# Feed-forward with context and latent tokens in tiles of their own, and tokens, weights and ring at one remainder modulo 512 bytes

## What is computed

```
h = rms_norm(x, norm2_gain) * (1.0 + sc2) + sh2
ff = square(relu(h @ w_ff1)) @ w_ff2
x = x + g2 * ff
y = rms_norm(x, final_gain)
```

## Time and profile before

| | |
|---|---|
| median of 3 runs | 1760.79 us (1759.97 to 1762.66) |
| the profiled execution's own time | 1762.74 us |
| its span, first to last instruction | 1761.0 us |
| TensorE busy | 1673.0 us, 95% |
| VectorE busy | 943.3 us, 54% |
| ScalarE busy | 650.0 us, 37% |

### The profile page before, as it was taken

How to read it: one execution, slowest core, us unless ns; L and a number is a source line. 1 busy time by engine, 2 the same in 40 slices (tenths; PEclk the granted TensorE clock), 3 DMA queues, 4 the chain that set the end, 5 groups by cost and what they waited for, 6 DMA issues and landing times.

```text
span 1761.0 us, 30968 instructions
## 1 busy us (share of the span) xinstructions
PE 1673.0 (95%) x13028; PEld 1399.8 (79%) x13028; DVE 943.3 (54%) x1355; ACT 650.0 (37%) x932; POOL 0.2 (0%) x4
## 2 busy tenths in 40 slices
PE   7799999889999999499999999999999999999997
PEld 5577787768777877497688888888878888888886
DVE  5712643653365346656686665666575444444436
ACT  3423236423643272417474445444442220122103
POOL 0000000000000000000000000000000000000000
PEclk7899999989999999699999999999999999999999
DMA  8454234323433243720052222222372220122102
GB/s 341 184 190 148 67 130 145 132 85 113 160 117 116 81 169 96 273 62 26 25 189 90 88 99 107 82 90 97 123 284 108 108 108 29 79 107 108 54 1 120
DMA packets 62270, 208.20 MB, mean 118 GB/s; under 512 B 8784, under 2 KB 17488, under 8 KB 60752
## 3 DMA queue, kind: packets, MB, share of 16 engines
q1 hardware_dynamic: 57120, 185.35, 29.1%
q10 hardware_dynamic: 5040, 21.22, 2.9%
HBM read 144.40 MB, written 62.13 MB: 117 GB/s over the span
## 4 chain that ended last, share of the span: by engine, by line
PE 49%; DVE 1%; DMA 1%; ACT 0%; issue 0%; SPq 0%; DVEq 0%
PE bank L95 16%; PE bank L97 16%; PE bank L96 16%; DMA hid_raw<-hidden 0%; PE bank L1269 0%; DVE hid_lo L1078 0%; DMA hidden<-c 0%; PE bank L711 0%; DVE x L1340 0%; DVE y_tok L1368 0%; DVE down_lo L1084 0%; DVE c L890 0%; DVE c L892 0%; PE bank L824 0%; SPq L1054 0%
## 5 line engine op out<-in xcount | busy, mean ns | idle before, releaser
L95 PE MATMUL bank<-h_hi,in_lo 128*128 128x512 f32 (+1 forms) x768 | 290.8, 379 | 12.1 <-issue 9.2
L96 PE MATMUL bank<-h_lo,in_hi 128*128 128x512 f32 (+1 forms) x768 | 277.8, 362 | 0.0
L95 PE MATMUL bank<-hid_hi,down_lo 128*128 128x512 f32 (+1 forms) x768 | 274.7, 358 | 3.0 <-DVE x L1340 1.5
L97 PE MATMUL bank<-h_hi,in_hi 128*128 128x512 f32 (+1 forms) x768 | 277.2, 361 | 0.0
L97 PE MATMUL bank<-hid_hi,down_hi 128*128 128x512 f32 (+1 forms) x768 | 273.1, 356 | 0.0
L96 PE MATMUL bank<-hid_lo,down_hi 128*128 128x512 f32 (+1 forms) x768 | 272.8, 355 | 0.0
L1340 DVE SCALAR_TENSOR_TENSOR x<-bank,mod,x 128x512 f32<-128x512 f32 (+1 forms) x216 | 142.1, 661 | 226.6 <-PE bank L97 226.5
L1698 ACT ACTIVATE mx_stage<-bank 128x512 f32<-128x512 f32 (+1 forms) x96 | 49.9, 523 | 351.8 <-PE bank L97 347.9
L95 PEld LDWEIGHTS bank<-h_hi,in_lo 128*128 128x128 f32 x768 | 149.1, 194 | 37.9 <-issue 14.9
L96 PEld LDWEIGHTS bank<-h_lo,in_hi 128*128 128x128 f32 x768 | 149.7, 195 | 24.4 <-issue 5.5
L97 PEld LDWEIGHTS bank<-h_hi,in_hi 128*128 128x128 f32 x768 | 149.4, 195 | 21.9
(11 more groups left out here) (233 smaller groups left out, 2601.3 us busy)
## 6 DMA issues: line engine op xcount, KB each, us to landing
proj<-mx_stage ACTq DMA_DIRECT2D x32, 640.0 KB, 5.7
hid_raw<-hidden SPq DMA_DIRECT2D x32, 640.0 KB, 7.1
in_raw<-in_w_in SPq DMA_DIRECT2D x32, 512.0 KB, 6.3
mx_ada_raw<-in_w_ada_rest SPq DMA_DIRECT2D x32, 512.0 KB, 5.1
up_raw<-in_w_ff SPq DMA_DIRECT2D x32, 512.0 KB, 4.3
hidden<-c SPq DMA_DIRECT2D x64, 256.0 KB, 2.0
down_raw<-in_w_ff SPq DMA_DIRECT2D x32, 512.0 KB, 7.2
ada<-in_w_ada SPq DMA_DIRECT2D x8, 1024.0 KB, 20.7
```

The costliest lines, as they stand in the source:

```text
L95: nc.tensor.matmul(out, w_lo, x_hi, start=start, stop=False)
L96: nc.tensor.matmul(out, w_hi, x_lo, start=False, stop=False)
L97: return nc.tensor.matmul(out, w_hi, x_hi, start=False, stop=stop)
```

## The change

No instruction is added, removed or moved on any engine. Only addresses of SBUF tiles change.

- `h2_hi` and `h2_lo` are each cut into a context tile (8 rows of 258 columns) and a latent tile (8 rows of 1024 columns). The context tiles are at 0 and 8.0625 KB, the latent ones at 16.125 and 48.125 KB.
- The ring tiles `hid2` to `hid7` and `down7` move up by 128 bytes, since `kb` now applies to them too.
- All readers and writers take the pair of tiles and pick one.

```
@@ -553,8 +553,6 @@
-    H = TOKENS + 2
-    AT = {0: 0, 1: CTX + 2}
@@ -579,8 +577,10 @@
-        self.h_hi, self.h_lo = at(nc, "h2_hi", [P, KT, self.H], F32R, 0), at(nc, "h2_lo", [P, KT, self.H], F32R, 40.0625)
-        self.h_raw = at(nc, "h2_raw", [P, KT, self.H], F32, 40.0625)
+        ctx, lat = [P, KT, CTX + 2], [P, KT, LAT]
+        self.h_hi = at(nc, "h2_ctx_hi", ctx, F32R, 0), at(nc, "h2_lat_hi", lat, F32R, 16.125)
+        self.h_lo = at(nc, "h2_ctx_lo", ctx, F32R, 8.0625), at(nc, "h2_lat_lo", lat, F32R, 48.125)
+        self.h_raw = at(nc, "h2_lat_raw", lat, F32, 48.125)
@@ -595,8 +595,8 @@
-        at_hid = lambda s: kb((120, 130)[s]) if s < 2 else 10 * (s - 2)
-        at_w = lambda s: (kb(168), kb(176), kb(140), kb(148), kb(156), kb(184), kb(192), 60)[s]
+        at_hid = lambda s: kb((120, 130)[s] if s < 2 else 10 * (s - 2))
+        at_w = lambda s: (kb(168), kb(176), kb(140), kb(148), kb(156), kb(184), kb(192), kb(60))[s]
@@ -641,15 +641,14 @@
     def columns(self, t, k, t0, n):
-        col = t0 if t0 < CTX else t0 + 2
-        return t[:, k, col:col + n]
+        return t[0][:, k, t0:t0 + n] if t0 < CTX else t[1][:, k, t0 - CTX:t0 - CTX + n]
...
-            return self.h_hi[:, rows, cols], self.h_lo[:, rows, cols]
+            return self.h_hi[1][:, rows, cols], self.h_lo[1][:, rows, cols]
@@ -771,7 +770,7 @@
-                             self.h_hi[:, k, 0:CTX + 2], self.h_lo[:, k, 0:CTX + 2], k == 0, k == KT - 1)
+                             self.h_hi[0][:, k, :], self.h_lo[0][:, k, :], k == 0, k == KT - 1)
@@ -792,9 +791,9 @@
-                t = slice(CTX + 2 + b * self.HALF, CTX + 2 + (b + 1) * self.HALF)
+                t = slice(b * self.HALF, (b + 1) * self.HALF)
                 last = exact_product(nc, g.bank[self.PLAIN_BANKS[s][b]][:, :], hi[:, s, cols], lo[:, s, cols],
-                                     self.h_hi[:, k, t], self.h_lo[:, k, t], k == 0, k == KT - 1)
+                                     self.h_hi[1][:, k, t], self.h_lo[1][:, k, t], k == 0, k == KT - 1)
```

More of the change, by code:

```diff
@@ L643, in columns @@
     def columns(self, t, k, t0, n):
-        col = t0 if t0 < CTX else t0 + 2
-        return t[:, k, col:col + n]
+        return t[0][:, k, t0:t0 + n] if t0 < CTX else t[1][:, k, t0 - CTX:t0 - CTX + n]
     def right(self, i):
-        a, b, first_half, last_half = slice(0, 4), slice(4, 8), slice(CTX + 2, CTX + 2 + self.HALF), slice(CTX + 2 + self.HALF, self.H)
+        a, b, first_half, last_half = slice(0, 4), slice(4, 8), slice(0, self.HALF), slice(self.HALF, LAT)
         rows, cols = {1: (a, first_half), 2: (b, first_half), 3: (b, last_half), 4: (a, last_half)}.get(i, (None, None))
         if rows is not None:
-            return self.h_hi[:, rows, cols], self.h_lo[:, rows, cols]
+            return self.h_hi[1][:, rows, cols], self.h_lo[1][:, rows, cols]
         return {5: (self.t_hi[0], self.t_lo[0]), 6: (self.t_hi[1], self.t_lo[1]), 7: (self.t_hi[2], self.t_lo[2])}[i]
@@ L681, in scalar_row @@
         if m == 0:
-            nc.scalar.activation(self.h_hi[:, :, self.SHIFT], g.mod[:, 24:32, :], ACT.Copy).then_inc(self.sh_hi, 1)
+            nc.scalar.activation(self.h_hi[0][:, :, self.SHIFT], g.mod[:, 24:32, :], ACT.Copy).then_inc(self.sh_hi, 1)
         for t0, n, c in SEGS:
@@ L695, in vector_row @@
             dve.wait_ge(self.sh_hi, 1)
-            nc.vector.tensor_tensor(self.h_lo[:, :, self.SHIFT], g.mod[:, 24:32, :], self.h_hi[:, :, self.SHIFT].bitcast(F32),
+            nc.vector.tensor_tensor(self.h_lo[0][:, :, self.SHIFT], g.mod[:, 24:32, :], self.h_hi[0][:, :, self.SHIFT].bitcast(F32),
                                     ALU.subtract).then_inc(self.sh_lo, 1)
@@ L1189, in combination_hi @@
             raw, hi = ((self.t_raw[i - 1], self.t_hi[i - 1]) if i < 4 else
-                       (self.h_raw[:, 0:4, CTX + 2 + self.HALF:], self.right(4)[0]))
+                       (self.h_raw[:, 0:4, self.HALF:], self.right(4)[0]))
             nc.scalar.activation(hi[:, :, :], raw[:, :, :], ACT.Copy).then_inc(self.t_hi_ready, 1)
@@ L1283, in vector @@
         t1, t2, t3 = self.t_raw
-        t4 = self.h_raw[:, 0:4, CTX + 2 + self.HALF:]
+        t4 = self.h_raw[:, 0:4, self.HALF:]
         def make(out, k, i, minus):
```

## The result

| | us |
|---|---|
| before, median of 5 runs | 1759.97 (1758.70 to 1762.66) |
| changed, median of 5 runs | 1750.58 (1747.72 to 1753.57) |
| ratio | 0.9941, 95% interval 0.9927 to 0.9954 |
| span of the profiled execution, before and after | 1761.0 and 1747.6 |

The change saves 9.4 us, a good half per cent. I had said 7.2 us and a time between 1751.3 and 1757.3. The direction and the mechanism held, and the size was too small.

What follows compares the result with a forecast made beforehand. TensorE was taken to bound all but the passage between up and down stages; 3.13 (up) + 0.24 (plain pair) + 2.98 + 0.62 + 0.24 (down) = 7.2 us, from 1760.79 to 1753.6 us, range 1751.3 to 1757.3.

Steps and rivals of the forecast that it cites:

- The bound and the cover: Up and down stages: TensorE is busy throughout and stays the bound; VectorE (237 of 377 us) and ScalarE (185) are not short.
- Two paces: 512-column matmuls: equal operand remainders modulo 512 bytes settle at 226.7 ns each, unequal ones stay at 231 to 234.
- Products 2 to 4: Up stage, 36 latent matmuls of a pair: run settled, 8.33 to 8.16 us, 0.17 saved a pair.
- the 258-column matmuls keep theirs, and a hand-over follows each context block: Up stage: context tiles keep old remainders; block 0 goes from 2.87 to 2.89 us, 0.02 lost a pair.
- Product 7: Up stage, after context block 1, reading t and s: shows the hand-over and stays at 2.76 us.
- Product 1: Up stage, 12 latent matmuls: becomes like product 7, 2.81 to 2.76 us, 0.05 saved a pair.
- The ring: Down stage, groups of four slots: every row at 6.90 us, from 6.993 and 6.926, saving 2.98 and 0.62 us.
- The last group: End of down stage: nine units of six go from 12.51 to 12.27 us, 0.24 saved; nothing counted behind them among transposes.
- The passage: Up to down stage, bound by a chain over VectorE, store and reload: still 40 us long, no gain counted.
- Half: Rival: settled pace holds in the ring but not the up stage; 3.84 us saved, 1757.0 us; chance 0.08.
- it doesn't do what it says: Rival: the remainder isn't the cause of the paces; time as before, 1760.8 us; chance 0.08.
- Slower: Rival: hand-over starts anew at each tile change, 2.6 us lost up, 5.1 down; 1768.5 us; chance 0.04.

Runs made afterwards that it cites:

- e4: Changed kernel with weight sums s 128 bytes above tokens, hid2 to hid5 256 and hid6, hid7 384 above their weights; product 5 2.80 us, slots 2 to 5 6.90 a row.
- e6: Changed kernel with s 256 bytes above tokens, hid2 to hid5 64 and hid6, hid7 256 above their weights; product 5 2.72 us, a row of slots 2 to 5 6.86.
- e5: Changed kernel with token tiles reordered, latent hi 64 bytes below its weights, latent lo equal; products 2 to 4 8.42 us, a pair 25.15 us.
- e2: Changed kernel with the ring tiles put back to their old places, only token tiles cut and moved; 1754.15 us, ratio to before 0.9972.
- e0_after_again: The changed kernel without an edit, run again beside the kernel before; 1750.57 us (6 runs) against 1761.50 (11 runs), ratio 0.9937.
- e3: Changed kernel with both up weight buffers and rstd_lat 128 bytes higher, latent tokens as they were; a pair takes 25.05 us.
- e1: Kernel before with only the ring tiles (hid2 to hid7, down7) moved up 128 bytes; 1755.38 us, ratio to before 0.9983.
- e7: Changed kernel with s 64 bytes above tokens, hid2 to hid5 32 and hid6, hid7 192 from their weights; product 5 2.80 us, last group's nine units 12.59.
- e9: Changed kernel with s 32 bytes above tokens, hid2 to hid5 96 and hid6, hid7 160 ahead of their weights; product 5 2.80 us, last group's nine units 12.65.

## Why the prediction was wrong in its size

**The bound and the cover: right.** TensorE stayed busy through the up and down stages, and no engine became the bound.

**Two paces: right; the period: wrong, without harm.** Products 2 to 4 in 8.16 us and rows in 6.90 came out to the last digit. But 256 bytes apart is as good as equal (e4, e6), so 256 is the period and not 512.

**The step that failed: "the 258-column matmuls keep theirs, and a hand-over follows each context block. Product 7 shows such a hand-over".** I argued that the context tiles keep their remainders modulo 512, and took their pace and the 2.76 us hand-over behind them as fixed. Both changed. Product 1 takes 2.72 us and not 2.76, product 7 takes 2.72 and not 2.76, and the context blocks take 2.863 each and not 2.89. A pair is 24.773 us and not 24.90: 14 x 0.127 = 1.8 us, nearly the whole gap between the 3.13 of the forecast and the pairs' 4.96. e5 shows that the nearer rows of the context tiles do it for context block 1 and product 7. For context block 0 near rows were not enough: in e5 it has them, behind products at 234 ns, and takes 2.89. Product 1 came out like product 7, as I had assumed, and so shares its gain. So the paces of unequal matmuls hang on the stream before them as well, and I had carried them over from another place in the pair. A remainder modulo 512 was all that I had of the address, and the trace before held nothing on context rows at another distance; the honest range for that term was wider than the 1 us that I gave the sum.

**The ring: mis-sized a little.** Groups 1 to 7 gave 3.78 us for 3.60. Group 1 had rows of 7.01 before where I had used 6.99, and the first row of group 2 had 6.95 where I had used 6.93. My split of a row was off inside the right sum: before, the twelve narrow matmuls of slots 2 to 5 took 1.42 us, 118 ns each and not 121, and the wide ones 232 ns and not 231. So the narrow ones lose 0.01 us a row and the wide ones gain about 0.1. The last group gave 0.42 for 0.24: its nine units 0.27, and the wide units among the transposes 0.15, where I counted nothing.

**The passage: the chain of VectorE's work there did keep its length, but I was wrong to expect the passage to be still.** It came out 0.89 us shorter in the profiled execution. The chain that ended last says where. Before, between the lines of the earlier trace rows:

```profile
1296.68 5.45 DMA hidden<-c
```

After:

```profile
1275.77 0.70 DVE c L959
...
1288.41 4.70 DMA hidden<-c
...
1295.26 8.19 DMA hid_raw<-hidden
```

VectorE's part up to the store is 12.65 us in one and 12.64 in the other; the store and the load took 0.85 us less. That is not the change: over the profiled executions of all these kernels group 0 took from 28.63 us (e2) to 31.39 (`e0_after_again`, the changed kernel itself), with no order by layout. In `e0_after_again` TensorE waits 1.7 us for one of VectorE's additions there, in the same kernel's first profile 0.6.

**The time against which it was made.** The start of the feed-forward layer, the first matmul of the plain pair, wanders more than all this. The instructions up to there are the same in every kernel, and it came at 883.15 us in the kernel before, at 880.12 and 884.19 in the two profiles of the changed kernel, and at 878.42 in e3 and 889.32 in e6. So a median of a few runs carries an error of about a microsecond, and those of the kernel before show it: 1760.79 of three runs, 1759.97 of five, 1759.88 of nineteen and 1761.50 of eleven. Of the 3.0 us between my 1753.6 and the measured 1750.58, 0.8 is the base and 2.2 the saving that I had missed. The lower side of my range left only 2.3 us for both, so on which side of its edge the time fell was luck; the missed saving was not.

**The rivals.** "Half" and "it doesn't do what it says" are out by e1, e2 and e3. The rule of the Trainium skill that was weighed there, in "TensorE: Matmul & The Clock Gate", section "Step-by-step: what each phase is for", says that loading the next weights takes nothing from the running matmul. The runs don't agree with it as the rival used it, since the place of the weights matters: with tokens fixed and only the weights moved by 128 bytes (e3), product 2 went from 2.72 to 2.80 us. Whether something is lost at distance 0 too, these runs don't tell. "Slower" did not happen, and neither did its mechanism, a hand-over that starts anew at each change of tile: products 2 to 4 kept 226.7 ns over two such changes. e5 has its pace of 234 ns, but from unequal operands.

## What to carry to other kernels

Where TensorE is the bound and weights are loaded anew for every matmul, compare the paces of matmuls of one shape over the stages: a difference of 2 to 3% at one clock can come from the places of the operands. Here placing weights and tokens at one remainder modulo 256 bytes, rows included, brought 512-column matmuls from 231 to 234 ns down to 226.7. Check both widths, since the best distance for 256 columns was another one, and read the gain from the starts in a steady stretch, which repeat to 0.01 us where medians of whole runs wander by more than the gain. When rows of a tile move nearer to each other, don't take the pace of matmuls at uneven remainders as fixed.

## What the runs showed of the hardware that I had not expected

- The pace of a float32 matmul with its own weight load depends on the distance of the two operands modulo 256 bytes: 226.7 ns at 0, 229 at 64, 233 to 234 at 32, 96, 128, 160, 192 and 224 for 512 columns. For 256 columns 64 is the best of the four that were tried (0, 32, 64, 96), 113.3 or 118 ns against 120 at 0.
- The pattern has a memory. After a change of width or of distance it needs one to eight matmuls to settle, and at 64 bytes two steady paces were seen for narrow matmuls, 113.3 and 118 ns, even behind wide matmuls of the same distance (e6, groups 3 and 1). In the two profiles of the changed kernel the pieces of a pair agree to 0.001 us in the mean over the pairs.
- For context matmuls at uneven remainders behind a settled product, 4096 bytes more between rows changed context block 1 from 2.863 to 2.895 us and product 7, with the hand-over behind that block, from 2.724 to 2.758. With near rows but an unequal product 5 before it, context block 1 took 2.88 to 2.89 us (e4, e7, e9).
